# Trunk of two layers on one core: another cut of the first stage into blocks, and sums at other places in the first heads

## The chip, the cores and the metric

One core of one Trainium2 chip runs the whole program in one launch. The metric is the device time of an execution in microseconds, lower is better. All times below are counted from the start of the profiled span.

## What is computed

Two layers on 256 latent and 256 context tokens of width 2048 (batch 1): first neighbourhood attention with 16 heads, then a bidirectional Mamba-2 mixer. Each layer modulates its normalised input by a shift, a scale and a gate, which come from a product of the condition with a 2048 x 6144 matrix:

```python
for i in range(DEPTH):                                  # DEPTH = 2
    norm_w, ada_w, ada_b, mixer = layers[i]
    mod = sc @ ada_w + ada_b                            # sc = silu(c)
    shift, scale, gate = jnp.split(mod[:, None, :], 3, axis=-1)
    mod_c = scc @ ada_w + ada_b                         # scc = silu(c_ctx), for the context
    shift_c, scale_c, gate_c = jnp.split(mod_c, 3)
    h = rms_norm(x, norm_w) * (1 + scale) + shift
    hc = rms_norm(ctx, norm_w) * (1 + scale_c) + shift_c
    y, yc = mixer(h, hc)
    x = x + gate * y
    if yc is not None:
        ctx = ctx + gate_c * yc
return rms_norm(x, final_norm_w)
```

The attention mixer projects `h` with `na_w_in` to queries, keys, values and a gate path (head by head, 128 columns each), takes a softmax over local scores with a bias and a mask together with scores against the context, and weighs the values.

## The kernel before

The program is written engine by engine, in the order in which each engine works; semaphores join them. All large products are made three times in float32r (high part by high part, high by low, low by high), which keeps float32 accuracy. So each weight tile passes ScalarE (its high part, `w_hi`) and VectorE (its low part, `w_lo`) before TensorE uses it.

**First stage.** The 16 groups of 128 rows of `h` (index `k`) are cut into five blocks by `BLOCKS`. For a block `c`, shift and scale of its columns need all 2048 rows of two column ranges of `na_ada_w`. They arrive in pieces of 1 MB, issued from the SP queue as two DMAs each (L432): two rows of 128 by 512 columns where a block is 4 wide, four rows by 256 columns where it is 2 wide. A wide block has 8 such pieces, a narrow one 4. There are 4 places for them, so SP waits on `s_ada_used` before each one from the fifth on (`sp.wait_ge(s_ada_used, n - 3)`). `AHEAD` and `BEHIND` say which of the 8 loads of the first weights (`load_first_weights`, L421) goes in the middle of a block's pieces and which behind them; one such load serves two `k`.

TensorE multiplies a piece by the condition (`mod_products(c, q)`, L1995), and after the last of a block turns the sums to columns (`mod_columns(c)`, L2008, which needs ScalarE's copy L821). VectorE makes the modulation (`modulation`, L1312, L1316), and then ScalarE (`h_high`, L796), GpSimd (L630, the context's slice) and VectorE (`h_full` L1323, low part L1345) make `h` for each `k` of the block. With it TensorE runs `first_tiles(c, p)` (L2022 to L2024): for each `k` two calls `p`, each three tiles of the first two heads by three products, 9 matmuls of 128x512. `norm_rows` (L1980) spreads the tokens' factors over the rows, behind which VectorE scales all of `x` (L1303, four instructions).

The order of TensorE's calls, like that of all other engines here, is written out by hand.

**First heads.** Behind the stage come heads 0 and 1 (`first_heads` on ScalarE and VectorE), whose tiles are mostly made by then, and a loop over heads 2 to 15. Beside the attention, three engines make the columns of the layers' other modulation vectors in parts: GpSimd loads a part of two rows by 512 columns (`load_ada(l)`, L605), VectorE multiplies and adds it for the latent tokens (`ada_part(l)`, L1415), ScalarE multiplies it for the context (`products(l)`, L858) and GpSimd adds these products (`add_products(l)`, L614, L620). Eight parts make a sum; two buffers hold the loads, so load `l` waits until part `l-2` was read by both engines. VectorE's softmax work for a head (L1361 to L1368, L1373 to L1379) and the low parts of the weights (`split_lo`, L357) stand between the parts in its order, and the probabilities of head `i` are turned by TensorE (`turn_probs`, L2092, L2096) after a projection of 48 matmuls (L373 to L377).

## Time and profile before

| | |
|---|---|
| median of 3 executions | 2076.57 us (2076.32 to 2077.63) |
| the profiled execution | 2077.76 us, its span 2075.9 us |
| TensorE, matmuls busy | 2017.7 us (97%) |
| VectorE busy | 1459.5 us (70%) |
| ScalarE busy | 967.6 us (47%) |
| GpSimd busy | 665.7 us (32%) |
| DMA | 349.23 MB, mean 168 GB/s |
| mean granted TensorE clock | 0.989 of 2.4 GHz |

The durations are those of one profiled execution. A row of a timeline gives the start, the time from the first start to the last end of what it merges, the engine, the line of the kernel and the operation with its count; in square brackets the idle time before it and what ended it.

### The profile page before, as it was taken

Reading aid. Unit: us, or ns where it says so; the run is one execution under the profiler, and the core shown is the slowest. Engines: PE = TensorE matmul, PEld = TensorE weight load, DVE = VectorE, ACT = ScalarE, POOL = GpSimd, SP = SyncE. Lnnn points to the kernel's source line nnn. Section 1 sums busy time; section 2 is a strip of 40 time slices with the busy share of each in tenths; the row PEclk is TensorE's granted clock in tenths of the full one; section 3 lists DMA queues with packets and bytes.
Section 4 is the critical chain, followed back from the end, with each engine's and each line's share of the span. In section 5 each row is a group of like instructions: output and inputs, shape, how many; then the busy total and the mean of one; then the engine's idle time right before and its main releaser. Section 6 shows DMA issues by size and latency. Waiting matters only on the chain.

```text
span 2075.9 us, 31012 instructions
## 1 busy us (share of the span) xinstructions
PE 2017.7 (97%) x10458; PEld 1674.5 (81%) x10458; DVE 1459.5 (70%) x2076; ACT 967.6 (47%) x1398; POOL 665.7 (32%) x568
## 2 busy tenths in 40 slices
PE   5998999999999999999999999999999999999998
PEld 3567888888888888878878888888888888888886
DVE  5248777777777777774348877787878787777544
ACT  3244444455444544453355445445444544456443
POOL 1035666556565655635200111111112111110011
PEclk7999999999999999999999999999999999999999
DMA  9996667666666666656353554554554645556654
GB/s 352 338 261 140 168 177 184 174 173 168 172 174 178 178 171 173 164 141 172 102 152 98 149 147 125 144 147 125 143 149 114 167 116 147 138 148 199 226 184 153
DMA packets 422706, 349.23 MB, mean 168 GB/s; under 512 B 13600, under 2 KB 366464, under 8 KB 422016
## 3 DMA queue, kind: packets, MB, share of 16 engines
q1 hardware_dynamic: 397552, 273.43, 46.0%
q0 software_dynamic: 19968, 70.26, 14.1%
q10 hardware_dynamic: 5136, 4.89, 0.7%
q8 instruction: 28, 0.46, 0.1%
q14 instruction: 22, 0.18, 0.0%
HBM read 344.21 MB, written 4.33 MB: 168 GB/s over the span
## 4 chain that ended last, share of the span: by engine, by line
PE 82%; DVE 7%; DMA 4%; ACT 3%; issue 3%; POOL 1%; SPq 0%; DVEq 0%; POOLq 0%; ACTq 0%
PE bank L373 21%; PE bank L377 20%; PE bank L375 20%; DMA arena<-in_na_ada_w_dram 3%; PE bank L2303 3%; PE bank L2305 2%; PE bank L2304 2%; DVE w_lo L357 2%; PE bank L2241 1%; DVE arena L1647 1%; PE bank L2222 1%; PE bank L2107 1%; PE bank L1995 1%; PE bank L2022 1%; PE bank L2236 1%
## 5 line engine op out<-in xcount | busy, mean ns | idle before, releaser
L373 PE MATMUL bank<-act_hi,w_hi 128*128 128x512 f32 (+1 forms) x2448 | 906.0, 370 | 11.5 <-DVE w_lo L357 7.0
L377 PE MATMUL bank<-act_hi,w_lo 128*128 128x512 f32 (+1 forms) x2448 | 888.6, 363 | 0.0
L375 PE MATMUL bank<-act_lo,w_hi 128*128 128x512 f32 (+1 forms) x2448 | 888.0, 363 | 0.0
L357 DVE TENSOR_TENSOR w_lo<-arena,w_hi 128x2048 fp32r<-128x2048 f32 x184 | 435.2, 2365 | 210.8 <-ACT w_hi L353 147.9
L373 PEld LDWEIGHTS bank<-act_hi,w_hi 128*128 128x128 f32 x2448 | 462.7, 189 | 97.3 <-issue 14.4
L377 PEld LDWEIGHTS bank<-act_hi,w_lo 128*128 128x128 f32 x2448 | 462.5, 189 | 73.6
L375 PEld LDWEIGHTS bank<-act_lo,w_hi 128*128 128x128 f32 x2448 | 463.2, 189 | 68.8
L620 POOL TENSOR_TENSOR acc<-acc,arena 128x512 f32<-128x512 f32 x224 | 328.5, 1467 | 126.5 <-ACT arena L858 117.2
L353 ACT ACTIVATE w_hi<-arena 128x2048 fp32r<-128x2048 f32 x138 | 263.8, 1911 | 84.5 <-PE bank L2305 78.2
L1415 DVE SCALAR_TENSOR_TENSOR arena<-arena,cond_c 128x512 f32<-128x512 f32 x240 | 249.4, 1039 | 63.9 <-DMA arena<-in_ssd_ada_w_dram 37.6
L858 ACT ACTIVATE arena<-arena,cond_c 128x512 f32<-128x512 f32 x256 | 171.3, 720 | 261.1 <-POOL acc L620 151.0
L1647 DVE SCALAR_TENSOR_TENSOR arena<-arena,convc 128x512 f32<-128x512 f32 (+1 forms) x192 | 154.0, 802 | 105.6 <-ACT arena L1043 92.4
L728 POOL TENSOR_TENSOR arena<-arena 128x1024 f32<-128x1024 f32 x32 | 76.5, 2392 | 469.3 <-ACT arena L1059 439.9
L1059 ACT ACTIVATE arena<-arena 128x1024 f32<-128x1024 f32 x32 | 33.9, 1060 | 206.0 <-DVE arena L1699 206.0
L2303 PE MATMUL bank<-w_hi,act_hi 128*128 128x512 f32 x256 | 101.1, 395 | 1.9 <-DVE w_lo L357 1.9
L2305 PE MATMUL bank<-w_hi,act_lo 128*128 128x512 f32 x256 | 99.8, 390 | 0.0
L2304 PE MATMUL bank<-w_lo,act_hi 128*128 128x512 f32 x256 | 99.7, 389 | 0.0
L717 POOL TENSOR_SCALAR_AFFINE_SELECT arena<-arena 128x256 f32<-128x256 f32 (+1 forms) x32 | 21.9, 717 | 206.5 <-ACT arena L1172 206.5
L901 ACT ACTIVATE w_hi<-arena 128x2048 fp32r<-128x2048 f32 x43 | 82.0, 1908 | 0.0
L605 POOL DMA_DIRECT2D arena<-in_ssd_ada_w_dram x96 | 68.3, 712 | 33.5 <-DVE arena L1415 25.9
L1048 ACT ACTIVATE arena<-arena 128x512 f32<-128x512 f32 (+1 forms) x48 | 28.6, 597 | 101.4 <-DVE arena L1647 101.4
L1072 ACT ACTIVATE arena<-arena 128x256 f32<-128x256 f32 x128 | 54.3, 495 | 24.2 <-POOL arena L717 24.2
(253 smaller groups left out, 2157.8 us busy)
## 6 DMA issues: line engine op xcount, KB each, us to landing
arena<-in_ssd_w_in_dram SPq DMA_DIRECT2D x81, 1024.0 KB, 6.0
arena<-in_na_w_in_dram SPq DMA_DIRECT2D x58, 1024.0 KB, 7.3
arena<-in_ssd_ada_w_dram POOLq DMA_DIRECT2D x96, 512.0 KB, 4.1
arena<-in_na_ada_w_dram SPq DMA_DIRECT2D x64, 512.0 KB, 8.0
arena<-in_ssd_w_out_dram SPq DMA_DIRECT2D x32, 1024.0 KB, 5.1
arena<-in_na_ada_w_dram POOLq DMA_DIRECT2D x32, 512.0 KB, 4.2
arena<-in_na_w_out_dram SPq DMA_DIRECT2D x16, 1024.0 KB, 6.3
arena<-cs_scr SPq DMA_DIRECT2D x64, 256.0 KB, 5.5
```

The source lines that it names most:

```text
L353: nc.scalar.activation(w_hi[:, n0 % 2, :], raw[slot], ACT.Copy).then_inc(s_hi, 1)
L357: nc.vector.tensor_tensor(w_lo[:, n0 % 2, :], raw[slot], w_hi[:, n0 % 2, :].bitcast(F32), ALU.subtract).then_inc(s_lo, 1)
L373: nc.tensor.matmul(out[:, 0:cols], hi[:, w], act_hi3[:, k, 0:cols], start=(k == 0), stop=False)
L375: nc.tensor.matmul(out[:, 0:cols], hi[:, w], act_lo3[:, k, 0:cols], start=False, stop=False)
L377: mm = nc.tensor.matmul(out[:, 0:cols], lo[:, w], act_hi3[:, k, 0:cols], start=False, stop=(k == KT - 1))
L620: nc.gpsimd.tensor_tensor(acc[:, :], acc[:, :], prod[:, h, :], ALU.add).then_inc(s_gp, 1)
L858: m = nc.scalar.activation(prod[:, h, :], ada_buf[l % 2][:, h, :], ACT.Copy, scale=cond_c[:, k, 1:2])
L1415: m = nc.vector.scalar_tensor_tensor(ada_acc, ada_buf[l % 2][:, h, :], cond_c[:, k, 0:1], ada_acc, ALU.mult, ALU.add)
L1647: m = nc.vector.scalar_tensor_tensor(u, xp[:, 0:segs, k:k + LAT], col(48 + 48 * k), u, ALU.mult, ALU.add)
L2303: nc.tensor.matmul(b[:, :], hi, w_hi[:, n % 2, w], start=(k == 0), stop=False)
L2304: nc.tensor.matmul(b[:, :], hi, w_lo[:, n % 2, w], start=False, stop=False)
L2305: mm = nc.tensor.matmul(b[:, :], lo, w_hi[:, n % 2, w], start=False, stop=(k == IT - 1))
```

## The change

`BLOCKS` has its narrow blocks at both ends now, (2, 4, 4, 4, 2) instead of (4, 4, 4, 2, 2), with new entries in `AHEAD` and `BEHIND` and a new order of TensorE's calls. GpSimd issues the first two loads of its sums behind all slices of the context. In the first heads ScalarE's product 3, VectorE's parts 2 and 3 and GpSimd's loads 4 and 5 stand earlier.

```diff
--- before.py
+++ after.py
@@ -12,6 +12,7 @@
 
 
 
+import itertools
 from contextlib import ExitStack, contextmanager
 
 import concourse.bass as bass
@@ -49,11 +50,11 @@
 PRE = 6
 PRE_BANK = (4, 5, 6, 7, 0, 1)
 PRE_AT = (0, 2, 4, 5, 1, 3)
-BLOCKS = ((0, 4), (4, 4), (8, 4), (12, 2), (14, 2))
+BLOCKS = ((0, 2), (2, 4), (6, 4), (10, 4), (14, 2))
 FIRST_K = [k0 for k0, _ in BLOCKS]
-ADA_USED = [2 * k0 if nk == 4 else 24 + 2 * (k0 - 12) for k0, nk in BLOCKS] + [32]
-AHEAD = (0, 2, 4, 6, None)
-BEHIND = (1, 3, 5, None, 7)
+ADA_USED = list(itertools.accumulate([0] + [2 * nk for _, nk in BLOCKS]))
+AHEAD = (0, 1, 3, 5, None)
+BEHIND = (None, 2, 4, 6, 7)
 N_OUT_A = 4 * HEADS
 N_DT = N_OUT_A + KT
 N_SSD = N_DT + 1
@@ -622,9 +623,6 @@
             for k in range(KT):
                 if k in FIRST_K:
                     pool.wait_ge(s_mod, FIRST_K.index(k) + 1)
-                if k == KT - 2:
-                    load_ada(0, None, True)
-                    load_ada(1, None, True)
                 if k >= 3:
                     pool.wait_ge(s_h, k - 2)
                 nc.gpsimd.tensor_scalar(hx[k % 3][:, LAT:TOK], xn_t[:, k, LAT:TOK], gain_a[:, 1, k:k + 1],
@@ -648,6 +646,8 @@
                 nc.gpsimd.tensor_tensor(bias, bias, mask[:, :].unsqueeze(1).broadcast_to([P, 6, GRID_W]),
                                         ALU.add).then_inc(s_bias, 1)
 
+            load_ada(0, None, True)
+            load_ada(1, None, True)
             pool.wait_ge(s_h, KT)
             load_bias(None)
             add_products(0, None)
@@ -656,11 +656,11 @@
             add_products(1, None)
             load_ada(3, None, True)
             add_products(2, None)
+            load_ada(4, None, True)
             load_bias(1)
-            load_ada(4, None, True)
             add_products(3, None)
+            load_ada(5, None, True)
             mask_bias(1)
-            load_ada(5, None, True)
             for l in range(4, 7):
                 add_products(l, None)
                 if l + 2 < 8:
@@ -921,11 +921,12 @@
                 nc.scalar.activation(k_hi, bank[1][:, :], ACT.Copy).then_inc(s_khi_k, 1)
                 products(2, Turn())
                 exp_scores(Turn())
+                products(3, Turn())
                 turned_probs(Turn())
                 act.wait_ge(s_used, 7)
                 nc.scalar.activation(v_t, bank[2][:, :], ACT.Copy).then_inc(s_free[0], 1)
                 next_hi(4, Turn(base=4))
-                for l in range(3, 8):
+                for l in range(4, 8):
                     products(l, Turn())
 
             first_heads()
@@ -1500,13 +1501,14 @@
                 query_low(bank[0], Turn(base=1))
                 key_low(bank[1], Turn(base=1))
                 softmax(none)
+                ada_part(2, none)
                 split_lo(dve, 7, none, 1)
                 normalise(none)
                 v_low(none)
-                ada_part(2, none)
+                ada_part(3, none)
                 probs_low(none)
                 split_lo(dve, 8, none, 0)
-                for l in range(3, 6):
+                for l in range(4, 6):
                     ada_part(l, none)
                 gate_o(none, backwards_free(o_t[:, 0, :]))
                 for l in range(6, 8):
@@ -2028,12 +2030,22 @@
                 if p % 4 == 3 and k < KT - 1:
                     mm.then_inc(s_kused, 1)
 
-            for q in range(8):
-                mod_products(0, q)
-                if q == 2:
-                    norm_rows()
+            mod_products(0, 0)
+            mod_products(0, 1)
+            norm_rows()
+            mod_products(0, 2)
+            mod_products(0, 3)
             mod_columns(0)
-            for c in (1, 2):
+            first_tiles(0, 0)
+            first_tiles(0, 1)
+            mod_products(1, 0)
+            mod_products(1, 1)
+            first_tiles(0, 2)
+            for q in range(2, 8):
+                mod_products(1, q)
+            mod_columns(1)
+            first_tiles(0, 3)
+            for c in (2, 3):
                 for q in (0, 2, 4, 6):
                     if q < 6:
                         first_tiles(c - 1, q)
@@ -2043,26 +2055,17 @@
                 first_tiles(c - 1, 6)
                 mod_columns(c)
                 first_tiles(c - 1, 7)
-            for q in range(2):
-                first_tiles(2, 2 * q)
-                first_tiles(2, 2 * q + 1)
-            mod_products(3, 0)
-            mod_products(3, 1)
-            for p in range(4, 6):
-                first_tiles(2, p)
-            mod_products(3, 2)
-            mod_products(3, 3)
-            first_tiles(2, 6)
-            mod_columns(3)
-            first_tiles(2, 7)
+            for p in range(3):
+                first_tiles(3, p)
             mod_products(4, 0)
             mod_products(4, 1)
-            first_tiles(3, 0)
+            for p in range(3, 5):
+                first_tiles(3, p)
             mod_products(4, 2)
             mod_products(4, 3)
-            first_tiles(3, 1)
+            first_tiles(3, 5)
             mod_columns(4)
-            for p in range(2, 4):
+            for p in range(6, 8):
                 first_tiles(3, p)
             for p in range(4):
                 first_tiles(4, p)
```

TensorE at the start of the stage, before and after. L1995 and L1997 are `mod_products`, L1980 and L1982 `norm_rows`, L2008 and L2010 `mod_columns`, and the next three lines are the products of one tile:

```order
L1963 MATMUL bank<-ident,plain 128x128 x32
L1995 MATMUL bank<-arena 32x512 x12
L1980 MATMUL bank<-plain,ones 128x128 x4
L1995 MATMUL bank<-arena 32x512 x20
L2008 MATMUL bank<-sel_mod,arena 128x4 x4
L2022 MATMUL bank<-act_hi,w_hi 128x512
L2023 MATMUL bank<-act_lo,w_hi 128x512
L2024 MATMUL bank<-act_hi,w_lo 128x512
```


```order
L1965 MATMUL bank<-ident,plain 128x128 x32
L1997 MATMUL bank<-arena 32x256 x16
L1982 MATMUL bank<-plain,ones 128x128 x4
L1997 MATMUL bank<-arena 32x256 x16
L2010 MATMUL bank<-sel_mod,arena 128x4 x2
L2024 MATMUL bank<-act_hi,w_hi 128x512
L2025 MATMUL bank<-act_lo,w_hi 128x512
L2026 MATMUL bank<-act_hi,w_lo 128x512
```


`norm_rows` stands behind two pieces instead of three, and the first tile behind 4 pieces instead of 8. TensorE in the second block after the change:

```order
L2024 MATMUL bank<-act_hi,w_hi 128x512
L2025 MATMUL bank<-act_lo,w_hi 128x512
L2026 MATMUL bank<-act_hi,w_lo 128x512
L1997 MATMUL bank<-arena 32x512 x24
L2010 MATMUL bank<-sel_mod,arena 128x4 x4
L2024 MATMUL bank<-act_hi,w_hi 128x512
```


The last six pieces of block 1 (24 matmuls) follow each other with no tile between them; before, every two pieces were followed by two calls of tiles.

VectorE in heads 0 and 1, before and after, from the softmax's scores (L1361, L1362) on; the parts are L1415 and L1416, the low parts of the weights L357 and L358, the normalisation L1373 to L1379 and L1374 to L1380:

```order
L1361 TENSOR_TENSOR bank<-bank,arena 128x256 x2
L1366 TENSOR_REDUCE small<-bank 128x1 x2
L1368 TENSOR_REDUCE small<-bank 128x2
L357 TENSOR_TENSOR w_lo<-arena,w_hi 128x2048
L1373 RECIPROCAL small<-small 128x4
L1376 TENSOR_SCALAR arena<-arena,small 128x512 x2
L1379 TENSOR_SCALAR arena<-arena,small 128x256 x2
L1398 TENSOR_TENSOR rounded<-bank,rounded 128x512
L1415 SCALAR_TENSOR_TENSOR arena<-arena,cond_c 128x512 x2
L1392 TENSOR_TENSOR rounded<-bank,rounded 128x512 x3
L357 TENSOR_TENSOR w_lo<-arena,w_hi 128x2048
L1415 SCALAR_TENSOR_TENSOR arena<-arena,cond_c 128x512 x6
```


```order
L1362 TENSOR_TENSOR bank<-bank,arena 128x256 x2
L1367 TENSOR_REDUCE small<-bank 128x1 x2
L1369 TENSOR_REDUCE small<-bank 128x2
L1416 SCALAR_TENSOR_TENSOR arena<-arena,cond_c 128x512 x2
L358 TENSOR_TENSOR w_lo<-arena,w_hi 128x2048
L1374 RECIPROCAL small<-small 128x4
L1377 TENSOR_SCALAR arena<-arena,small 128x512 x2
L1380 TENSOR_SCALAR arena<-arena,small 128x256 x2
L1399 TENSOR_TENSOR rounded<-bank,rounded 128x512
L1416 SCALAR_TENSOR_TENSOR arena<-arena,cond_c 128x512 x2
L1393 TENSOR_TENSOR rounded<-bank,rounded 128x512 x3
L358 TENSOR_TENSOR w_lo<-arena,w_hi 128x2048
```


Part 2 stands now before the weights' low part and the normalisation, part 3 before the probabilities' low part (L1392, L1393).

GpSimd in the same heads, before and after, from sum 1 on; the loads are L605 and L606, the bias loads L643 and L641, the masked bias L648 and L646, the sums L620 and L621:

```order
L620 TENSOR_TENSOR acc<-acc,arena 128x512 x2
L605 DMA arena<-in_na_ada_w_dram 128x2x512
L620 TENSOR_TENSOR acc<-acc,arena 128x512 x2
L643 DMA arena<-in_na_rpb_dram 64x6x64 x2
L605 DMA arena<-in_na_ada_w_dram 128x2x512
L620 TENSOR_TENSOR acc<-acc,arena 128x512 x2
L648 TENSOR_TENSOR arena<-arena,mask 128x384
L605 DMA arena<-in_na_ada_w_dram 128x2x512
L620 TENSOR_TENSOR acc<-acc,arena 128x512 x2
L605 DMA arena<-in_na_ada_w_dram 128x2x512
```


```order
L621 TENSOR_TENSOR acc<-acc,arena 128x512 x2
L606 DMA arena<-in_na_ada_w_dram 128x2x512
L621 TENSOR_TENSOR acc<-acc,arena 128x512 x2
L606 DMA arena<-in_na_ada_w_dram 128x2x512
L641 DMA arena<-in_na_rpb_dram 64x6x64 x2
L621 TENSOR_TENSOR acc<-acc,arena 128x512 x2
L606 DMA arena<-in_na_ada_w_dram 128x2x512
L646 TENSOR_TENSOR arena<-arena,mask 128x384
L621 TENSOR_TENSOR acc<-acc,arena 128x512 x2
L606 DMA arena<-in_na_ada_w_dram 128x2x512
```


Load 4 went ahead of the bias loads, and load 5 ahead of the masked bias.

## Rows read from the trace of the kernel before

**Rows 1.** The chain that ended last, 30 to 210 us: start us, us, what.

```profile
64.23 7.23 DMA arena<-in_na_ada_w_dram
...
177.54 4.61 DMA arena<-in_na_ada_w_dram
...
186.19 3.99 DMA arena<-in_na_ada_w_dram
```

**Rows 2.** Timeline of TensorE, 20 to 155 us: start us, us, line, operation, count [idle before].

```profile
22.94 4.43 PE L1995 MATMUL bank<-arena 128*32 128x512 f32 x24 [2.40 <-DVE col_d L1290]
...
41.83 1.94 PE L1995 MATMUL bank<-arena 128*32 128x512 f32 x8 [0.79 <-DMA arena<-in_na_ada_w_dram]
...
49.03 0.79 PE L2022 MATMUL bank<-act_hi,w_hi 128*128 128x512 f32 x1 [2.68 <-DVE act_lo L1345]
...
55.47 1.92 PE L1995 MATMUL bank<-arena 128*32 128x512 f32 x16
...
57.32 0.50 PE L2022 MATMUL bank<-act_hi,w_hi 128*128 128x512 f32 x1
...
61.67 1.92 PE L1995 MATMUL bank<-arena 128*32 128x512 f32 x16
...
78.30 0.50 PE L2022 MATMUL bank<-act_hi,w_hi 128*128 128x512 f32 x1 [0.48 <-DVE act_lo L1345]
...
142.25 0.66 PE L2022 MATMUL bank<-act_hi,w_hi 128*128 128x512 f32 x1 [2.69 <-DVE w_lo L1328]
...
152.12 0.60 PE L2115 MATMUL bank<-ident,arena 128*128 128x128 f32 x4
```

**Rows 3.** Timeline of TensorE, 160 to 205 us.

```profile
165.61 1.03 PE L2092 MATMUL bank<-ident,arena 128*128 128x128 f32 x8
...
199.13 1.97 PE L2092 MATMUL bank<-ident,arena 128*128 128x128 f32 x8 [5.54 <-DVE arena L1379]
...
201.60 0.78 PE L373 MATMUL bank<-act_hi,w_hi 128*128 128x512 f32 x1
```

**Rows 4.** Timeline of VectorE, 18 to 50 us.

```profile
28.56 8.88 DVE L1303 TENSOR_TENSOR arena<-bank,arena 128x2048 f32<-128x2048 f32 x4 [4.11 <-issue]
...
37.36 1.75 DVE L1328 TENSOR_TENSOR w_lo<-arena,w_hi 128x1536 fp32r<-128x1536 f32 x1
...
46.39 0.37 DVE L1312 TENSOR_TENSOR mod_a<-bank,colk 128x4 f32<-128x4 f32 x4 [7.28 <-PE bank L2008]
```

**Rows 5.** Loads of the modulation weights (L432), issued 56.5 to 58.6 us.

```profile
L432 SPq DMA_DIRECT2D arena<-in_na_ada_w_dram x4: 368/468/472, 56.6 to 58.0; - x4
...
DMA to landing us min/median/max: 4.2/5.6/6.8
```

**Rows 6.** Busy by engine, 56 to 58 us; last: granted clock, DMA share, GB/s.

```profile
56.00:58.00 2.00, 2.00 (x19) 0.76 (x12) 0.00 (x0) 0.00 (x0) 0.00 (x0) 1.00 0.18 24
```

**Rows 7.** Timeline of GpSimd, 130 to 140 us.

```profile
136.30 1.62 POOL L605 DMA_DIRECT2D arena<-in_na_ada_w_dram  x2 [9.79 <-DVE gain_a L1316]
```

**Rows 8.** Timeline of VectorE, 130 to 140 us.

```profile
138.61 0.69 DVE L1345 TENSOR_TENSOR act_lo<-arena,act_hi 128x512 fp32r<-128x512 f32 x1 [2.17 <-POOL arena L630]
```

**Rows 9.** Timeline of ScalarE, 140 to 150 us.

```profile
148.91 0.60 ACT L909 ACTIVATE rounded<-bank 128x512 fp32r<-128x512 f32 x1 [4.65 <-PE bank L2024]
```

**Rows 10.** Timeline of GpSimd, 160 to 190 us.

```profile
166.04 0.72 POOL L605 DMA_DIRECT2D arena<-in_na_ada_w_dram  x1 [4.75 <-DVE arena L1415]
...
172.29 3.88 POOL L620 TENSOR_TENSOR acc<-acc,arena 128x512 f32<-128x512 f32 x2 [5.53 <-ACT arena L858]
...
183.60 2.66 POOL L620 TENSOR_TENSOR acc<-acc,arena 128x512 f32<-128x512 f32 x2 [1.65 <-ACT arena L858]
```

**Rows 11.** Timeline of VectorE, 160 to 200 us.

```profile
163.09 0.61 DVE L1379 TENSOR_SCALAR arena<-arena,small 128x256 f32<-128x256 f32 x2
...
190.21 1.54 DVE L1415 SCALAR_TENSOR_TENSOR arena<-arena,cond_c 128x512 f32<-128x512 f32 x2 [1.40 <-DMA arena<-in_na_ada_w_dram]
...
198.46 0.61 DVE L1379 TENSOR_SCALAR arena<-arena,small 128x256 f32<-128x256 f32 x2
```


## Prediction

> **What bounds the kernel now.** I read the busy shares first, then the chain of work that ended last, then the timelines of the engines in the two places that the change touches. TensorE is busy for 97% of the span, so time is to be had only where it waits or runs at its lower clock. The chain names such places. Before 80 us it passes through the transfers of the modulation weights (7.23 us ending at 71.46), and at 177 to 190 us through two loads of GpSimd's sums [rows 1]. In the timeline of TensorE the first tile starts at 49.03; from then to the end of the stage at 152.12 it waits only in small pieces and once for 2.69 us, at 142.25 [rows 2]. Later one wait stands out: 5.54 us at 199.13, for head 2's probabilities [rows 3]. After it the heads show no wait of note. The change works on exactly these stretches: the start, the 2.69 us, and the 5.54 us.
>
> I call the 32 pieces of 1 MB in which the modulation weights arrive slabs 0 to 31. Four places hold them, so slab n is issued only when TensorE has used slab n-4.
>
> **Part 1, the five blocks.** *The start.* The row of squares' factors now goes behind two slabs instead of three; three took 4.43 us [rows 2], so it comes 1.45 us sooner, and VectorE's scaling of all of x, 8.88 us long and ending at 37.44 [rows 4], ends at 36.0. The low part of the first weights (1.75) follows: 37.75. From the start of the modulation to the first tile it is 49.03 - 46.39 = 2.64 us [rows 2, 4]. First tile: **40.4** instead of 49.03. The columns no longer hold it up, as slabs 2 and 3 come in long before 36. On the SP queue as many bytes stand in as many DMAs as before, eight slabs in the narrow shape again; only the loads of first weights change places among them, each before the tile that needs it, so I set that at nothing (between a slab's pitch, 2.7, early or late for one tile).
>
> *What it costs.* At 40.4 only 4 slabs are used, where at 49.03 it was 8. Two tiles come first, 18 matmuls in 55.47 - 49.03 = 6.44 us from a cold start [rows 2], then slab 4 (0.93): 47.8. Only now may slab 8 be issued. Its transfer was free to start much sooner, so the queue runs dry. The trace has this very gap once already: slab 12 is issued at 56.59, when TensorE has come to slab 8, and in 56 to 58 the queues move 24 GB/s [rows 5, 6]. A half slab landed 4.2 us after issue at best, the second half about 1.4 later [rows 5], so slab 8 is there at 47.9 + 5.6 = 53.5, and the next three each 0.79 + 1.94 = 2.73 us later [rows 2]: 61.7 for slab 11. Meanwhile TensorE has one tile and little else to do.
>
> After slab 11 there are its product (0.93 warm, 1.94 cold), the copy, the columns and the modulation: from the end of slab 7's product, 43.77, to the first tile, 49.03, it was 5.26 us [rows 2]. The one tile left of block 0 lies in it, about 2.1 us warm and 3.8 cold. That gives block 1's first tile at **67.2** if the clock has held, and **69.4** if it has fallen, since the columns, the product and this tile are then slower.
>
> *The rest by counting.* Before, 24 tiles and 16 slabs were left at 78.30, and took 152.12 - 78.30 = 73.8 us with all waits [rows 2]. Now 28 tiles and 20 slabs are left. Two more pairs of tiles cost 2 x (61.67 - 57.32) = 8.7, two more pairs of slabs 2 x (57.32 - 55.47) = 3.7, wider columns 0.45: 86.7 us. End of the stage: 153.9 warm, 156.1 cold, against 152.12. A further wait for slab 19, whose transfer carries the early gap along, is bounded by nothing from below and by a slab's pitch less a product, 1.8, from above; I take 0.9, the middle.
>
> **Part 2, the loads behind the slices.** In the last block GpSimd issued two loads (1.6 us) ahead of its slices, and VectorE waited 2.17 us for the first slice [rows 7, 8]. Without them ScalarE's two halves and its weights set the pace: I get the last tiles 0.8 us sooner, with a wait of about 2 in place of 2.69 us. What becomes late are the two loads themselves, 1.4 us. ScalarE's products of them were followed by a wait of 4.65 us, up to 148.91 [rows 9], and this covers them: cost nothing, or 1.4 without that cover.
>
> Parts 1 and 2: 1.8 + 0.9 - 0.8 = 1.9 warm, 4.0 + 0.9 - 0.8 = 4.1 cold. The cold case is a little likelier: TensorE would wait four times between 53 and 62, about 1.8 us each; behind a wait of 2.69 us the clock was down, behind waits under 1 us it was not [rows 2]. I take **+3.3 us**.
>
> **Part 3, the first heads.** The 5.54 us come from a chain. GpSimd issued load 4 at 166.04 after waiting 4.75 us for VectorE's part 2; its sum 3 ran 3.88 us from 172.29, because ScalarE's product came late [rows 10]; load 5 went out at 177.54, load 7 at 186.19 with 3.99 us on the way [rows 1]; part 7 ran at 190.21, and only behind it did VectorE do head 2's softmax, ending with probabilities at 198.46 + 0.6 [rows 11]. Now part 2 stands ahead of the low part of the weights and of the normalisation (about 4.8 us of VectorE), so load 4 leaves at 161.2; product 3 and part 3 are moved ahead too (ScalarE was idle there, so nothing queues behind its product), and load 5 passes the masked bias: 167.5. The bias of head 1 is not needed before head 2's scores. Then part 4, behind the weights of the next tile as before, limits load 6 (175.3), and the sum 5 load 7 (179). With 4.0 us on the way, part 7 starts near 183 instead of 190.21, 7.2 us sooner, and the probabilities at 191.9. TensorE needs them at 199.13 - 5.54 = 193.6. The slack is 1.7 us.
>
> Worth: 5.54, and the low clock after the wait. The transposes take 201.60 - 199.13 = 2.47 us there; the first eight of them need 1.97 against 1.03 in head 1 [rows 3], so 1.2 us of this is the clock, and the next five matmuls lose 1.0. Together 7.7. From below it is nothing, if something else holds the probabilities. The price on the other side: in head 1 the probabilities are ready 1.5 us (part 2) later, at 163.7 + 1.5 = 165.2 [rows 11], where TensorE came for them at 165.61 [rows 3]. I leave 0.3 for that: **-7.4 us**.
>
> **Rules weighed.** Sum 3 took 3.88 us beside VectorE's parts, sum 5 took 2.66 without them [rows 10]. The Trainium skill, SBUF - State Buffer (on the shared port pair), says that VectorE reading two SBUF operands and a reading GpSimd instruction exclude each other. By that rule three sums now beside VectorE's parts would take up to 1.2 us more each; this is rival B. [...]
>
> **The sum.** 3.3 - 7.4 = **-4.1 us**. The profiled execution took 2077.76 (span 2075.9), 1.2 over the median of 2076.57; the durations hold for either. Predicted: 2076.57 - 4.1 = **2072.5**. What can be told from no change is 0.2%, 4.15 us, so this lies on the border.
>
> **Rivals.**
> - *A, the clock holds while TensorE waits for slabs 8 to 11.* For it: waits under 1 us did not lower it. Against: four in a row. Stage +1.9 and a little less behind the last wait: -6 us, **2070.5**. Chance 0.24.
> - *B, GpSimd's sums slow down beside VectorE.* Three times 1.2 us make part 7 3.6 us late against a slack of 1.7, and the loads that follow leave later still, say 0.6: a wait of about 2.5, which as at 142.25 brings the low clock [rows 2]. Of 7.4 some 3.5 remain: **2076.4**. For it the 3.88, against it the 2.66. Chance 0.13.
> - *C, slower: the transfers starve again.* Slab 16 is issued when TensorE has used slab 12, 5.1 us after block 1's first tile; the queue is dry near 75. If that tile starts after about 70, there is a second gap, then a third; each costs about 3 us as at 54 to 60 and 1 to 2 of low clock. Two of them: +8.6, **2081.1**. For it: 69.4 is close. Against: slabs 12 to 15 and a tile's weights stand in the queue ahead of slab 16. Chance 0.13.
> - *D, the stage gains.* If the early tiles take up waits that I have counted twice, the stage ends 1 us sooner: **2068.2**. Chance 0.08.
>
> The forecast has 0.42. It alone spans 2070.5 to 2074.5. The range 2068.5 to 2079.0 leaves out C and about half of D. Faster by over 0.2%: 0.19 of the forecast, 0.21 of A, 0.08 of D: 0.48. Slower: C, 0.13. The rest is 0.39.
>
> **What would show it.** First tile near 40.4; a dry stretch of the queues near 44 to 49; waits for slabs 8 to 11; the clock in 55 to 68; the stage's end near 155; part 7 near 183 after the shift of the stage; no wait at head 2's transposes. I am wrong if the stage ends before 152, if the queues run dry again after 70, or if head 2 still waits over 1 us.

## The result and the profile after

| | before | after |
|---|---|---|
| median | 2077.34 us (2075.82 to 2080.68, 14 runs) | 2081.74 us (2080.34 to 2084.23, 14 runs) |
| the profiled execution | 2077.76, span 2075.9 | 2081.71, span 2079.9 |

The ratio is 1.0019, with a 95% interval of 1.0011 to 1.0027: the change makes the kernel about 4 us slower. I had predicted 4.1 us faster, with a range that ended at 2079.0. Both large terms of the sum failed. The stage ends 6.2 us later instead of 3.3, and the first heads give back 1.4 us instead of 7.4.

The first view is TensorE's timeline from 20 to 160 us (line numbers of this kernel are 2 or 3 above those of before).

```profile
39.48 0.80 PE L2024 MATMUL bank<-act_hi,w_hi 128*128 128x512 f32 x1 [3.08 <-DVE act_lo L1346]
...
52.07 1.06 PE L1997 MATMUL bank<-arena 128*32 128x512 f32 x8 [0.54 <-DMA arena<-in_na_ada_w_dram]
54.78 1.07 PE L1997 MATMUL bank<-arena 128*32 128x512 f32 x8 [1.65 <-DMA arena<-in_na_ada_w_dram]
57.49 1.93 PE L1997 MATMUL bank<-arena 128*32 128x512 f32 x8 [1.64 <-DMA arena<-in_na_ada_w_dram]
61.02 1.94 PE L1997 MATMUL bank<-arena 128*32 128x512 f32 x8 [1.60 <-DMA arena<-in_na_ada_w_dram]
...
69.39 0.63 PE L2024 MATMUL bank<-act_hi,w_hi 128*128 128x512 f32 x1
...
148.50 0.47 PE L2024 MATMUL bank<-act_hi,w_hi 128*128 128x512 f32 x1 [1.85 <-DVE w_lo L1329]
...
158.34 0.60 PE L2118 MATMUL bank<-ident,arena 128*128 128x128 f32 x4
```

The first tile comes at 39.48 instead of 49.03, and slabs 8 to 11 each have a wait ahead of them. At 57.49 a product takes 1.93 us where at 54.78 it took 1.07: the clock has fallen. Block 1's first tile is at 69.39. The last tiles wait 1.85 us instead of 2.69. The stage ends at 158.34; before it was 152.12 [rows 2].

The busy times by stretch of 10 us say why. Behind the stretch and its length stand the busy us of TensorE's matmuls, its weight loads, VectorE, ScalarE and GpSimd, each with its count; the last three columns are the granted clock (1.00 is 2.4 GHz), the DMA share and GB/s.

```profile
40.00:50.00 10.00, 10.00 (x47) 6.19 (x49) 2.23 (x2) 1.49 (x1) 0.00 (x0) 0.85 0.54 171
50.00:60.00 10.00, 5.59 (x40) 0.78 (x32) 0.00 (x0) 0.00 (x0) 0.00 (x0) 0.84 1.05 387
60.00:70.00 10.00, 8.26 (x27) 5.56 (x28) 3.46 (x12) 4.34 (x9) 3.57 (x4) 0.50 1.07 375
70.00:80.00 10.00, 10.00 (x52) 6.74 (x50) 3.21 (x4) 1.69 (x2) 0.00 (x0) 0.98 0.88 295
```

From 40 to 50 the DMA engines are only half used, while TensorE works on tiles and holds all four places. Then the queues are full and TensorE is busy for 5.59 of 10 us, and the clock is at its lower level, 0.50, all through 60 to 70. From 70 to 80 the queues run dry again, if for less long: 128 GB/s from 74 to 76, where from 44 to 46 it was 0. SP's own timeline has both gaps, between its loads of first weights and the next slab: 37.4 to 46.6, and up to 75.20.

```profile
34.21 3.23 SPq L422 DMA_DIRECT2D arena<-in_na_w_in_dram  x4
46.58 6.05 SPq L433 DMA_DIRECT2D arena<-in_na_ada_w_dram  x8
```

```profile
75.20 1.90 SPq L433 DMA_DIRECT2D arena<-in_na_ada_w_dram  x4
```

In the heads, TensorE's timeline has three waits where there was one of 5.54 us [rows 3].

```profile
173.55 1.09 PE L2095 MATMUL bank<-ident,arena 128*128 128x128 f32 x8 [1.62 <-DVE arena L1380]
...
202.28 1.09 PE L2095 MATMUL bank<-ident,arena 128*128 128x128 f32 x8 [0.70 <-DVE arena L1380]
...
229.87 0.50 PE L374 MATMUL bank<-act_hi,w_hi 128*128 128x512 f32 x1 [2.16 <-DVE w_lo L358]
```

The first is head 1's probabilities. VectorE's timeline there:

```profile
165.62 1.96 DVE L1416 SCALAR_TENSOR_TENSOR arena<-arena,cond_c 128x512 f32<-128x512 f32 x2
167.50 2.28 DVE L358 TENSOR_TENSOR w_lo<-arena,w_hi 128x2048 fp32r<-128x2048 f32 x1
...
169.91 3.06 DVE L1377 TENSOR_SCALAR arena<-arena,small 128x512 f32<-128x512 f32 x2
```

Part 2 takes 1.96 and not 1.5, and the pair of 128x512 in the normalisation takes 3.06 us. In head 2 of this kernel the same pair takes 0.88. On GpSimd, sum 3 starts at the same moment:

```profile
169.95 2.73 POOL L621 TENSOR_TENSOR acc<-acc,arena 128x512 f32<-128x512 f32 x2
```

The third wait, for `w_lo` of head 2's second projection, has a chain behind it, in the timelines of GpSimd and then ScalarE:

```profile
207.22 1.01 POOL L646 TENSOR_TENSOR arena<-arena,mask 128x384 f32<-128x384 f32 x1 [7.10 <-DMA arena<-in_na_rpb_dram]
208.20 3.33 POOL L615 TENSOR_TENSOR acc<-arena 128x512 f32<-128x512 f32 x1
211.47 0.72 POOL L606 DMA_DIRECT2D arena<-in_na_ada_w_dram  x1
```

```profile
211.56 1.34 ACT L858 ACTIVATE arena<-arena,cond_c 128x512 f32<-128x512 f32 x2 [6.09 <-POOL acc L615]
218.96 1.34 ACT L858 ACTIVATE arena<-arena,cond_c 128x512 f32<-128x512 f32 x2 [6.06 <-DMA arena<-in_na_ada_w_dram]
223.50 1.34 ACT L858 ACTIVATE arena<-arena,cond_c 128x512 f32<-128x512 f32 x2 [3.19 <-POOL acc L621]
...
225.22 1.91 ACT L901 ACTIVATE w_hi<-arena 128x2048 fp32r<-128x2048 f32 x1
```

GpSimd stands 7.10 us for the bias of the loop's head to land. The first sum and load 2 are queued behind that, ScalarE's products wait for both, and the high part of the next weights stands behind the products. Before, TensorE had lost 5.5 us at head 2's transposes, and so came late enough for this chain.

### The profile page after: what moved, and what is told of

It is laid out like the page before. It is cut to its first block, busy times and chain, and to the rows that moved or that the text cites. A ratio compares the mean times of both kernels' runs of the same rounds, so it can differ in the third digit from the quotient of the medians.

```text
span 2079.9 us, 31011 instructions
## 1 busy us (share of the span) xinstructions
PE 2016.7 (97%) x10458; PEld 1674.8 (81%) x10458; DVE 1458.2 (70%) x2076; ACT 968.0 (47%) x1398; POOL 663.1 (32%) x568
## 4 chain that ended last, share of the span: by engine, by line
PE 82%; DVE 8%; ACT 3%; issue 3%; DMA 3%; POOL 1%; SPq 0%; DVEq 0%; ACTq 0%; POOLq 0%
PE bank L374 21%; PE bank L378 21%; PE bank L376 21%; PE bank L2306 3%; PE bank L2308 2%; PE bank L2307 2%; DVE w_lo L358 2%; DMA arena<-in_na_ada_w_dram 2%; DVE arena L1649 2%; PE bank L2244 1%; PE bank L2110 1%; PE bank L2225 1%; PE bank L2024 1%; PE bank L2239 1%; PE bank L2082 1%
## 5 line engine op out<-in xcount | busy, mean ns | idle before, releaser
L358 DVE TENSOR_TENSOR w_lo<-arena,w_hi 128x2048 fp32r<-128x2048 f32 x184 | 432.5, 2351 | 214.3 <-ACT w_hi L354 147.8
L621 POOL TENSOR_TENSOR acc<-acc,arena 128x512 f32<-128x512 f32 x224 | 330.3, 1475 | 114.3 <-ACT arena L858 105.0
L1416 DVE SCALAR_TENSOR_TENSOR arena<-arena,cond_c 128x512 f32<-128x512 f32 x240 | 248.4, 1035 | 58.7 <-DMA arena<-in_ssd_ada_w_dram 38.0
L606 POOL DMA_DIRECT2D arena<-in_ssd_ada_w_dram x96 | 68.4, 712 | 35.4 <-DVE arena L1416 29.9
```

What stands on the lines that cost most here:

```text
L358: nc.vector.tensor_tensor(w_lo[:, n0 % 2, :], raw[slot], w_hi[:, n0 % 2, :].bitcast(F32), ALU.subtract).then_inc(s_lo, 1)
L621: nc.gpsimd.tensor_tensor(acc[:, :], acc[:, :], prod[:, h, :], ALU.add).then_inc(s_gp, 1)
L1416: m = nc.vector.scalar_tensor_tensor(ada_acc, ada_buf[l % 2][:, h, :], cond_c[:, k, 0:1], ada_acc, ALU.mult, ALU.add)
```

## The experiments

Two milestones are read from each profiled execution: the end of the stage (the row of 128x128 x4 behind the tiles, 152.12 before, 158.34 after) and from there the way to head 3's transposes (251.17 - 152.12 = 99.05 us before; 255.99 - 158.34 = 97.65 after). Each edit is given against the kernel that its sentence names; every ratio is to the kernel before, with its 95% interval.

**The three parts alone.** The edits are the parts of the diff above, each applied to the kernel before.

Part 1:

> Only part 1 of the change (blocks 2, 4, 4, 4, 2 with TensorE's order and the loads of the first weights). Theory of the trace after (the stage starves twice): first tile near 39.5, waits for slabs 8 to 11 of 1.6 us each, a second dry stretch of the queues at 70 to 80, end of the stage 5.5 to 7.5 us later than 152.1, and the whole kernel 5 to 7 us slower than the kernel before. The prediction's figure for this part was +4.1 (3.3 and the 0.8 that part 2 takes off). Rival: the stage by itself costs little and its late end came from part 2 or the sums; then the whole is within 2 us of the kernel before.

Ratio 1.0036 (1.0022 to 1.0049), some 7.5 us slower. Waits of 1.64, 1.66 and 2.10 us for slabs 9 to 11, slab 16 issued at 75.23, end of the stage 158.54, the way to head 3 98.70. The theory holds, though its 5 to 7 us were a little low: this part alone loses more than the whole change does.

Part 2:

> Only part 2 (GpSimd's first two loads behind its slices). Theory: the last tiles wait about 1.9 us instead of 2.69 and the stage ends 0.8 us sooner; the loads land 1.4 us later, which ScalarE's long wait covers; whole kernel 0 to 1.5 us faster. Rival: the later loads push the chain of sums, part 7 comes 1.4 us later and the gain is given back at head 2's wait; then the kernel is the same within 0.5 us and the 5.54 us wait grows to about 7.

Ratio 0.9992 (0.9983 to 1.0001): too little to tell from no change. The wait is 1.85, the wait at head 2 stays 5.53, so the later loads cost nothing; the stage ends at 151.98.

Part 3:

> Only part 3 (the sums' early parts in the first heads). The prediction's figure was -7.4 us. Theory of the trace after: head 1's probabilities come late (new wait of 1.5 to 2 us), head 2's wait falls from 5.54 to under 1, and head 2's next weights bring a new wait near 2 us with a low clock behind it; then the whole is only 1 to 3 us faster. Rival: these new waits came from the later stage, and here most of the 7.4 us are won.

Ratio 0.9983 (0.9974 to 0.9992), 3.5 us faster and not 7.4. The new waits are there without any change in the stage: 1.56, 0.68 and 2.42 us, and the low clock behind the last. The rival falls. VectorE's pair takes 3.05 us here too. In the profiled execution the way to head 3 is only 1.2 us shorter (97.82). It would be some 1.6 us shorter still without the low clock behind the last wait, which is not there in every execution (below).

Parts 2 and 3 together:

> Parts 2 and 3 on the old blocks, no part 1. If the parts add up as measured one by one, about 4 to 5 us faster than the kernel before (0.9977 to 0.9983), and the new waits are those of the changed kernel: some 1.6 us at head 1's probabilities, under 1 at head 2's, 2 to 2.4 at head 2's second projection. Rival: the loads behind the slices, 1.4 us late, add to the chain of sums only when the sums are early; then the gain is under 3 us.

Ratio 0.9979 (0.9970 to 0.9988), 4.4 us faster. The waits are 1.56, 0.21 and 2.03. With part 1's 0.36% this adds up to +0.15%, where the change measured +0.19%.

**TensorE uses slabs 4 to 7 early.** Against the changed kernel:

```diff
             mod_products(0, 3)
+            mod_products(1, 0)
+            mod_products(1, 1)
             mod_columns(0)
+            mod_products(1, 2)
             first_tiles(0, 0)
+            mod_products(1, 3)
             first_tiles(0, 1)
-            mod_products(1, 0)
-            mod_products(1, 1)
             first_tiles(0, 2)
-            for q in range(2, 8):
+            for q in range(4, 8):
                 mod_products(1, q)
```

> The changed kernel with TensorE's products of slabs 4 and 5 ahead of block 0's columns and those of slabs 6 and 7 ahead of its first two calls of tiles, so that places are free some 8 us sooner. Theory (the stage loses because the queue runs dry while TensorE has not used slabs 4 to 7): slab 8 is issued near 39 instead of 46.6, the four waits of 1.6 us shrink, and the second dry stretch at 70 to 80 goes too; first tile up to 3 us later than 39.5; stage ends 2 to 5 us sooner than 158.3. Rival (the loss is in the larger count of bytes ahead of the tiles, not in the order): the stage ends within 1 us of 158.3.

Ratio 0.9972 (0.9960 to 0.9985), 6 us faster than before, and some 10 us faster than the change with the same blocks (1.0019 less 0.9972). Busy times by stretch in this version:

```profile
40.00:50.00 10.00, 9.20 (x31) 4.36 (x32) 4.48 (x11) 3.56 (x5) 1.19 (x2) 0.53 1.07 372
50.00:60.00 10.00, 9.28 (x61) 5.25 (x60) 0.76 (x7) 0.75 (x2) 0.09 (x1) 1.00 1.02 348
60.00:70.00 10.00, 9.49 (x49) 6.12 (x48) 5.92 (x9) 5.28 (x9) 3.48 (x4) 1.00 1.03 362
70.00:80.00 10.00, 10.00 (x61) 5.79 (x59) 1.76 (x1) 1.48 (x1) 0.00 (x0) 1.00 1.06 380
```

The queues are full in all four stretches, 372 GB/s in the first where the change had 171. SP issues slab 8 at 38.44. The first tile is 3.7 us later, and block 1's first tile 7.6 us sooner:

```profile
43.20 0.80 PE L2024 MATMUL bank<-act_hi,w_hi 128*128 128x512 f32 x1 [0.81 <-DVE act_lo L1346]
...
61.82 0.50 PE L2024 MATMUL bank<-act_hi,w_hi 128*128 128x512 f32 x1 [0.51 <-DVE act_lo L1346]
```

The stage ends at 153.84 in this execution, which met two waits of 1.6 us and a low clock at 80 to 90, and at 148.54, 149.83 and 150.09 in the three versions below with the same stage. Even with full queues the last slabs of blocks 2 and 3 still come late, with waits of 1.10 to 1.33 us and 0.89 to 1.09 in those three. The rival, that the bytes and not the order cost the time, falls.

**Which sum slows the normalisation.** In the changed kernel, one sum cut to a column, which leaves out the rest of that sum:

```diff
-                    nc.gpsimd.tensor_tensor(acc[:, :], acc[:, :], prod[:, h, :], ALU.add).then_inc(s_gp, 1)
+                    w = 1 if i is None and l == 3 else 512
+                    nc.gpsimd.tensor_tensor(acc[:, 0:w], acc[:, 0:w], prod[:, h, 0:w], ALU.add).then_inc(s_gp, 1)
```

I first cut the wrong one, `l == 2`:

> The changed kernel with GpSimd's sum of part 2 in the first heads cut to one column of 512 (this leaves out part of one sum, so the second layers' modulation is not computed). Theory (GpSimd's sum and VectorE's normalisation hold each other up): VectorE's pair of 128x512 in head 1 takes 0.9 us instead of 3.06, head 1's probabilities are 2.2 us sooner and the wait of 1.62 us is gone. Rival (the normalisation is slow for a reason of its own, such as what stands ahead of it on VectorE): it still takes about 3 us. The time of the whole: 1 to 4 us faster than the changed kernel.

One run, 2080.79 us. The pair took 3.09 us, because sum 2 is over before it; sum 3 is what runs beside it (170.84 to 173.6). It is not a plain miss: part 2 of VectorE, which sum 2 does run beside, took 1.53 instead of 1.96, and head 1's wait was 1.15. Then `l == 3`:

> The changed kernel with GpSimd's sum of part 3 in the first heads cut to one column of 512 (part of one sum is left out). It is sum 3, not sum 2, that runs beside head 1's normalisation; thinning sum 2 left the pair at 3.09 us. Theory (the sum of 128x512 on GpSimd and the pair on VectorE hold each other up): the pair takes 0.9 us, head 1's wait of 1.62 us falls to nothing, and GpSimd's load 5 leaves about 2 us sooner after the start of head 1. Rival (the pair is slow because of what stands ahead of it on VectorE): still 3.1 us, wait still 1.6.

VectorE's timeline of that run:

```profile
169.43 2.28 DVE L358 TENSOR_TENSOR w_lo<-arena,w_hi 128x2048 fp32r<-128x2048 f32 x1
171.63 0.17 DVE L1375 RECIPROCAL small<-small 128x4 f32<-128x4 f32 x1
171.84 0.90 DVE L1378 TENSOR_SCALAR arena<-arena,small 128x512 f32<-128x512 f32 x2
```

The pair takes 0.90 us and the wait at head 1's transposes is gone. The theory holds for VectorE; the sum itself had not been held up (2.73 us beside the pair, 2.67 for sum 2). But the wait at head 2's transposes stayed 0.75 and the one for `w_lo` 2.23, and the one run measured 2080.24, as the fastest of the changed kernel (2080.34). The trace does not show the removed wait being paid again up to head 3: the two later waits kept their size, and the way to head 3 was 254.71 - 160.28 = 94.43 us in place of 97.65. Of these 3.2 us some 1.6 are the clock, which stayed high behind the wait for `w_lo` here, and 1.6 are the wait. But this run's stage ended 1.9 us later than the change's, so one run's time says nothing on it. Load 5 left 5.8 us behind load 4 instead of 8.0.

**The masked bias later in the loop.** Against the changed kernel:

```diff
                 load_bias(i)
-                mask_bias(i)
                 add_products(0, i)
-                for l in range(2, 8):
+                load_ada(2, i, gate)
+                mask_bias(i)
+                add_products(1, i)
+                for l in range(3, 8):
                     load_ada(l, i, gate)
                     add_products(l - 1, i)
```

> The changed kernel, and in the loop over heads GpSimd's masked bias behind the first sum and load 2. Theory: head 2's wait of 2.16 us for w_lo and the low clock behind it go, 2.2 to 3.7 us less than the changed kernel, which comes out near the kernel before (ratio 1.0002 to 1.0010). Rival: head 2's wait is only moved to a later head or projection; ratio as for the changed kernel, 1.0019.

Ratio 1.0012 (1.0003 to 1.0021), just outside the theory's 1.0002 to 1.0010. The wait for `w_lo` is gone and no later one took its place up to head 3, but here head 2's transposes waited 1.92 us, with the low clock behind it; the way to head 3 is 96.40 us in place of 97.65. This longer wait is not the work of the edit, which stands behind it in GpSimd's order: VectorE's last parts, beside a sum, took until 197.54 from 193.88, 3.66 us, where in the change it was 2.38 (192.85 to 195.23). So the wait at head 2's transposes varies by more than 1 us between traces of the same first heads. By the time the gain, 0.7 us between the medians and 1.5 by the ratios, is inside the interval. The same edit on the version that uses slabs early:

> The version that multiplies slabs 4 to 7 early, and in the loop over heads GpSimd's masked bias behind the first sum and load 2 instead of ahead of them. Theory (the 2.1 us wait in head 2 comes from GpSimd waiting 7 us for the bias to land, with the sum, ScalarE's products and its next high part queued behind): ScalarE's products in head 2 run 5 to 7 us sooner, the wait for w_lo near 225 is gone, 2 us less, up to 3.5 with the low clock: ratio near 0.996 of the kernel before. Rival (load 2's own way decides): the wait stays over 1 us and the time is that of the version without this edit.

Ratio 0.9966 (0.9954 to 0.9978), against 0.9972 without the edit, which the intervals don't part. No wait for `w_lo`; head 1's is 1.60, head 2's transposes don't wait at all, and the way to head 3 is 241.54 - 148.54 = 93.00 us. In ScalarE's timeline the high part comes 13.8 us sooner (225.22 in the change), 9.8 of it from the stage:

```profile
211.40 1.90 ACT L903 ACTIVATE w_hi<-arena 128x2048 fp32r<-128x2048 f32 x1
```

**Are the new blocks worth anything?** The kernel before with parts 2 and 3 and the masked bias later:

> Parts 2 and 3 on the old blocks (no part 1), with the masked bias behind the first sum and load 2. It tells what the new blocks are worth when TensorE frees the places early: theory (the new blocks cost only by the starvation, and without it give about 1 us): this is 0 to 1.5 us slower than the version with the new blocks and slabs 4 to 7 multiplied early, ratio 0.9966 to 0.9973. Rival (the old blocks are better in any order): faster than that, ratio under 0.9962.

Ratio 0.9967 (0.9956 to 0.9979), as the theory had it, though the interval doesn't exclude the rival's 0.9962. With the places freed early the new blocks are neither better nor worse by the time. This stays open within some 2 us: with part 2 the stage ended at 149.33, 151.75 and 151.98 in three versions with the old blocks, and at 148.54, 149.83, 150.09 and 153.84 in four with the new ones. 1.6 us of such differences is the clock behind the last tiles' wait, which stayed high in the runs with 149.33, 148.54 and 153.84 and fell in the others.

The masked bias later made the time shorter in all three pairs of versions, by 0.06, 0.07 and 0.12% (0.9979 with parts 2 and 3 alone, 0.9967 here). No pair shows it by itself, as each lies inside its intervals.

**Two other orders in head 1.** VectorE's normalisation ahead of the low part of the weights, on the version that uses slabs early:

```diff
-                split_lo(dve, 7, none, 1)
                 normalise(none)
+                split_lo(dve, 7, none, 1)
                 v_low(none)
```

> The version that multiplies slabs 4 to 7 early, with VectorE's normalisation of head 1 ahead of the low part of the next weights. Theory: it runs before GpSimd's next sum begins, the pair takes 0.9 us, the probabilities are over 3 us sooner, and TensorE's wait of 1.55 us is gone; the low part of the weights ends 2 us before TensorE needs it; 1.5 to 2 us faster than without this edit, if head 2's probabilities do not take it back. Rival: TensorE, sooner by 1.5 us, meets a longer wait at head 2's transposes or weights, and the time stays within 0.5 us.

Ratio 0.9970 (0.9958 to 0.9982), against 0.9972 without: nothing. Head 1's wait went, and head 2's probabilities came 2.08 us late instead of 0.26. The collision had only moved, if the wait at head 2 is not the varying one seen above. Now the low part runs beside the sum, and both are slow, 4.13 us on VectorE (2.28 in the changed kernel) and 4.62 on GpSimd (2.73):

```profile
159.19 1.11 DVE L1377 TENSOR_SCALAR arena<-arena,small 128x512 f32<-128x512 f32 x2
...
160.81 4.13 DVE L358 TENSOR_TENSOR w_lo<-arena,w_hi 128x2048 fp32r<-128x2048 f32 x1
```

```profile
161.48 4.62 POOL L621 TENSOR_TENSOR acc<-acc,arena 128x512 f32<-128x512 f32 x2
```

GpSimd's sum 3 behind load 5, with the masked bias later:

```diff
             load_bias(1)
+            load_ada(5, None, True)
             add_products(3, None)
-            load_ada(5, None, True)
             mask_bias(1)
```

> New blocks with slabs 4 to 7 multiplied early, the masked bias later in the loop, and GpSimd's sum of part 3 in the first heads behind load 5, so that it does not run beside head 1's normalisation. Theory: the pair takes 0.9 us, head 1's wait of 1.6 us goes, nothing takes its place because load 5 leaves sooner too: 1.5 us less than without this edit, ratio near 0.9958. Rival: the sum then runs beside the low parts and slows those (a low part of 128x2048 took 4.13 us beside a sum in the version with the normalisation first), and head 2's probabilities come late: ratio 0.9966 or more.

Ratio 0.9964 (0.9951 to 0.9977), level with the version without this edit. The pair takes 0.88 and head 1 has no wait, but head 2's transposes wait 2.54. The rival holds in what it says of the place: the low part of the next weights takes 2.96 (2.29 in the change), sum 4 takes 4.54, load 6 leaves 12.1 us behind head 1's transposes (163.58 to 175.64) instead of 11.5 (173.55 to 185.02 in the change, and 11.5 as well in the version without this edit), and VectorE's last parts before head 2's softmax, which met a sum again, take 3.70:

```profile
183.42 3.70 DVE L1418 SCALAR_TENSOR_TENSOR arena<-arena,cond_c 128x512 f32<-128x512 f32 x2 [1.40 <-DMA arena<-in_na_ada_w_dram]
```

The best versions, with medians of 2069.34 and 2069.81, are by their ratios some 7 us faster than the kernel before and 11 faster than the change.

## Why the prediction was wrong

**Part 1, the start, was right; what followed was undersized.** Forecast and trace: first tile 40.4 and 39.48; first gap of the queues 44 to 49, and 0 and 14 GB/s from 44 to 46 and 46 to 48; slab 11's product at 61.7 and 61.02; block 1's first tile 69.4 with the clock fallen, and 69.39. That the last pair agrees so closely is in part luck: from slab 11's product to this tile I had 7.7 us and it was 8.4. Two steps failed.

- *"I take +3.3"*, a value between a warm and a cold case. The waits for slabs 8 to 11 did bring the clock down to 0.50, its level of 1.2 GHz. It was still high for slab 9's product, behind waits of 0.54 and 1.65, and low from slab 10's on, behind a third one of 1.64. So the cold case held, which gives +4.1 by the same working. I had the reason for it in the text, and averaged it away.
- *"The rest by counting"*, with 0.9 for *"A further wait for slab 19"*. From 69.39 to the end I had 86.7 + 0.9 - 0.8 = 86.8 us and it was 88.95. Slab 19 waited 1.58, not 0.9, and slab 27 1.34, where the count held the 0.80 of the old slab 23. About half of the missing 2.2 us is the second dry stretch of the queues, which I had given to rival C: in the two versions with full queues and the same low clock behind the last tiles' wait, this way took 87.94 (61.89 to 149.83) and 87.78 us (62.31 to 150.09), with 1.33 and 1.18 at slab 19 and 0.95 and 0.89 at slab 27. The other 1 us is missing from the count even without that stretch; 0.3 to 0.4 of it is slab 19, and what makes up the rest stays open. Slab 16 was issued at 75.20, and C had put the dry spot "near 75". C's condition was a tile after about 70, and my own cold case stood at 69.4: I called it close and still kept the two apart, where the one is the other's mild form. C's price of about 3 us and 1 to 2 of low clock for each gap was too high; TensorE had tiles to work on, and the second gap cost about 1 us. That C's 2081.1 lies 0.6 us from the measured median is luck: it is the sum of two gaps at 4.3 us each and of a full gain in the heads, and neither was there.

**Part 2 was right**: the wait of 1.85 against "about 2", and no cost of the later loads.

**Part 3, -7.4 us, was the larger error.** Alone it gave -3.5 (0.9974 to 0.9992). Counted from the end of the stage, load 4 left 9.5 us on (forecast 9.1), load 5 17.5 (15.4), load 6 26.7 (23.2) and load 7 30.4 (26.9); before, load 7 left at 34.1. Part 7 came 34.5 us on instead of 30.9, so it was 3.6 us sooner and not 7.2, and used up what the prediction put as "The slack is 1.7 us"; only because head 1's wait had made TensorE late too, the wait left at head 2 was no more than 0.70. The 5.54 us and some 2.1 of low clock behind them did go (from head 2's transposes to head 3's first row 38.6 us before, and in the change 40.3 less 2.16 and 1.6). In return came waits of 1.62, 0.70 and 2.16 and 1.6 of low clock, 6.1 in all, which leaves about the 1.4 that was read. Three steps failed.

- *"in head 1 the probabilities are ready 1.5 us (part 2) later"*, with *"I leave 0.3 for that"*. They were 3.6 us later from the end of the stage: 1.96 for part 2 and 2.2 for the pair of the normalisation, less 0.5 of a faster low part. That made the wait of 1.62 us, and the late transposes in turn held VectorE's low parts and with them part 4 and loads 6 and 7.
- *Rival B, the sums slow down beside VectorE.* The collision was right and its victim wrong. I priced it on GpSimd's sums and not on VectorE's normalisation, whose two instructions took 3.06 us together, the first of them 1.65. The Trainium skill, SBUF - State Buffer (on who interferes with whom), names two kinds of VectorE instruction that contend with GpSimd: those with two SBUF inputs, and those in a 2-port mode, which tensor_scalar can enter; whoever issues first holds the port for a whole instruction. I had used the first kind only, and the second speaks of just this pair. The trace agrees on the kind: each instruction of the pair took about as long as one half of GpSimd's sum (2.73 / 2 = 1.4), and with the sum cut to a column both together took 0.90. On who waits it does not show the rule at work: by the rows the pair starts 0.04 us before the sum (169.91 and 169.95) and is still the one that is slow.
- *"Worth: 5.54, and the low clock after the wait."* I took the whole wait as gain and never asked what came next. The stall had been the cover of a chain behind the bias of head 2. With the stall gone that chain became a wait of 2.0 to 2.4 us in the change, in part 3 alone and in four more versions. In the version with the normalisation first, where head 2's transposes waited 2.08 us again, it was only 0.54: a stall covers it. With the masked bias later it was gone in all four versions that did so, and in two of them without any such cover (no wait and one of 0.77 us at head 2's transposes).

The sum, by the trace: 6.2 us in the stage, less 1.4 in the heads, less 0.8 spread behind head 3, gives the 4.0 between the spans.

## What to carry over

When early work takes the engine that frees a ring of buffers, count the ring as well: the transfers stop when the last place is full, so the uses that free places go ahead of the new work if they can run. Before a stall is booked as gain, follow every engine past it to the next thing that TensorE needs; what the stall covered is the price. A piece moved on VectorE is to be laid beside GpSimd's timeline, and with it all that it pushes back.

## What the runs showed of the hardware

- A pair of 128x512 tensor_scalar on VectorE took 0.88 us, and 3.05 to 3.09 us beside a GpSimd sum of two 128x512 that itself stayed at 2.73 to 2.74. A low part of 128x2048, with two inputs from SBUF, took 2.28, and beside such a sum 4.13, and there the sum took 4.62. Which of the two loses differs with the kind of instruction.
- The same short wait did not always bring the lower clock. Behind the last tiles' wait of 1.85 us the way to the end of the stage was 9.84 us in the change (148.50 to 158.34) and 8.29 in the version that uses slabs early (145.55 to 153.84), for the same instructions. Behind the wait for `w_lo` in head 2 the way to head 3's first row was 12.66 and 12.64 us after waits of 2.16 and 2.42 (the change, part 3 alone), and 11.02 to 11.04 after waits of 2.03, 2.06, 2.15 and 2.23 in four other versions, where the clock stayed at 1.00. Some 1.6 us hang on this each time, which is the size of several effects above; only the timed runs average over it.
